# A place in TensorE's order: the second half's norm sums stand at the second slab behind a mixer, and one short unit further on behind a feed-forward

## Chip, core and metric

One NeuronCore of a Trainium2 chip runs the whole program in one launch. The metric is the device time of that launch in microseconds (us); less is better. "TensorE" is PE in the profile's rows (PEld are its weight loads), "VectorE" DVE, "ScalarE" ACT, "GpSimd" POOL, and SP issues the weight stream's DMAs.

## What is computed

Five transformer layers on 512 tokens of width 1024, all in float32. Four layers have a mixer (differential attention, gated linear recurrence, sliding-window attention, differential attention) and a feed-forward, and each of the two is followed by a layer norm over the 1024 features; then a gate adds an embedding. A fifth layer has RMS norms. Cut to what matters here:

```python
def layer_norm(x, g, b):
    mu = jnp.mean(x32, axis=-1, keepdims=True)
    var = jnp.mean(jnp.square(x32 - mu), axis=-1, keepdims=True)
    y = (x32 - mu) * lax.rsqrt(var + LN_EPS) * g + b
...
    for i in range(DEPTH):                      # 4
        y = mixer_i(h)                          # ends in @ w_out
        h = layer_norm(ALPHA * h + y, ln_g[i, 0], ln_b[i, 0])
        u = jnp.square(jax.nn.relu(h @ w_up[i])) @ w_down[i]
        h = layer_norm(ALPHA * h + u, ln_g[i, 1], ln_b[i, 1])
        h = h + jax.nn.sigmoid(h @ w_ple_gate[i]) * (p[i] @ w_ple[i])
# second block: rms_norm, many projections and a merge, @ w_out, rms_norm, feed-forward, rms_norm
```

## The kernel before

**Layout and precision.** Activations lie with features across the 128 partitions: `h[128, 8, 512]` is 8 chunks of 128 features by 512 tokens. A float32 product is made from three matmuls with the operands split in a high and a low part: `whi*xh + whi*xl + wlo*xh` (L446 to L448 for 512 tokens, L545 to L547 for half of them).

**The weight stream.** SyncE streams the weights as slabs of 1024 x 256 into a ring (`raw<-in_stream`). For each slab GpSimd makes the high part (`high_part`, L424, `whi<-raw`) and VectorE the low part (`low_parts`, L1586, `wlo<-raw,whi`), which raises the semaphore `split_done`. A *unit* is TensorE's work on one slab. `begin_unit` waits for `split_done` of the unit's slab, and for the release of the PSUM banks that the unit before last used.

**The order of the work** is written out by hand, engine by engine; there is no scheduler. Each engine runs its own list in order, and a wait holds all that stands behind it on its engine.

**A norm** runs on two halves of the tokens (256 each), so that TensorE has work meanwhile. `pair(..., made=l)` runs the last two units ahead of norm `l` half by half: both units' first halves, then both units' second halves; each half is 8 chunks of 6 matmuls of 256 columns ("half-matmuls" below). `pair(..., read=l)` does the same with the first two units (slabs) that read what norm `l` makes. For each half, the steps are:

- VectorE adds the units' results into `h` and adds up `s1` (sum of `h`) and `s2` (sum of squares, ScalarE squares) with `sums` (L1692);
- TensorE's `stats` (L522) adds `s1` and `s2` across partitions with one-column matmuls; it waits for the semaphores `s1_added` and `s2_added`;
- VectorE's `norm_scalars` (L1700 to L1713) makes mean and reciprocal deviation, with one square root on ScalarE (L1056), and raises `norm_ready`;
- TensorE's `spread` (L533) waits for `norm_ready` and spreads the two rows over the partitions;
- VectorE (L1725, L1727), ScalarE (L1064, L1067) and GpSimd (L419, `xl<-h,xh`) apply them in five pieces of 1, 1, 2, 2, 2 chunks. In an RMS norm VectorE does GpSimd's part (L1743, L1751).

The first half's pieces let `pair(read=l)` do its units' first halves (semaphores `half_x` or `half_r`, a wait per chunk); the second half's pieces (`xh_ready`, `xl_ready`, a wait at every second chunk) let it do the second halves. VectorE's own list at a border (function `border`) is, for the second half:

```python
half(3, 1)                  # add the last unit's second half into h
sums(l, 3, 1)
low_parts(base + 5)         # wlo of the slab of pair(read)'s second unit
norm_scalars(l, 1)
apply(1, 0)
apply(1, 1)
```

GpSimd's list there has the last three pieces of the first half, then `whi` of the slab after (`base + 6`), then the second half's pieces.

There are eleven norms. Norms 0, 2, 4, 6 stand behind the mixers; `pair(read=0, 2, 4, 6)` reads them. Norms 1, 3, 5, 7 stand behind the feed-forwards; behind them TensorE has four short units, all on one slab: those of `p @ w_ple` (12 matmuls of 512 columns each, L446 to L448 with `ph`), and then the gate's units, which read the norm. Norm 8 stands behind the fourth layer's gate, norm 9 behind the second block's `w_out`, norm 10 ends the program. The change touches `pair` (L548) and the loop over the short units (L865 to L870).

Of the kernel before, what the change touches and what calls it, by code (L numbers as in the profile page):

```python
# [193 lines left out]
def build(nc, stream, xin, pin, pos, vecs, relb, onehot, eye, swap, picks, decay, resets, out):  # L194
    with ExitStack() as ctx:
# [168 lines left out]
        def M(name):  # L364
            if name not in m:
                m[name] = sem(name)
            return m[name]
# [74 lines left out]
        def _(pe):  # L442
# [7 lines left out]
            def begin_unit(u):  # L450

                if u:
                    pe.wait_ge(split_done, PLAN.unit_slab[u] + 1)
                if u >= 2:
                    e, v = PLAN.released(u - 2)
                    pe.wait_ge(rel[e], v)
# [27 lines left out]
            def operand_wait(which, gen, k):  # L484

                if k % 2 == 0:
                    hi, lo = (xh_ready, xl_ready) if which == "x" else (gh_ready, gl_ready)
                    pe.wait_ge(hi, gen * 4 + k // 2 + 1)
                    pe.wait_ge(lo, gen * 4 + k // 2 + 1)
# [3 lines left out]
            def whole_unit(u, which, gen=None, token=False, kn=8, w0=0, operand=None):  # L493
                begin_unit(u)
                op = operand or (X if which == "x" else G)
                for k in range(kn):
                    if gen is not None:
                        operand_wait(which, gen, k)
                    last = token_chunk(u, k, kn, op) if token else feature_chunk(u, k, kn, w0, op)
                last.then_inc(unit_done, 1)  # L500

            def out_chunks(layer, first, end):

                for i in range(first, end):
                    j, k = TAIL[i]
                    u = PLAN.at[f"out{layer}"][1] + j
                    if k == 0:
                        begin_unit(u)
                    operand_wait("x", X_GEN[f"mix{layer}"], k)
                    last = feature_chunk(u, k, 8, 0, X)  # L510
                    if k == 7:
                        last.then_inc(unit_done, 1)

            def stats(l, hf):

                for q, total, sem_ in ((0, s1, M("s1_added")), (1, s2, M("s2_added"))):
                    if q == 0 and l >= 2 * NL:
                        continue
                    pe.wait_ge(sem_, 5 * l + (5 if hf else 3))
                    for t in range(2 * hf, 2 * hf + 2):  # L520
                        for part in range(2):
                            last = nc.tensor.matmul(mix[:, 0, 4 * q + t:4 * q + t + 1], total[:, part, t * P:(t + 1) * P], ones[:, 0:1],  # L522
                                                    start=part == 0, stop=part == 1, skip_group_check=True)
                last.then_inc(M("stats"), 1)

            def spread(l, hf):

                pe.wait_ge(M("norm_ready"), 2 * l + hf + 1)
                for bank, c in ((2, 208), (3, 212)):
                    if bank == 3 and l >= 2 * NL:  # L530
                        continue
                    for t in range(2 * hf, 2 * hf + 2):
                        last = nc.tensor.matmul(mix[:, bank, t * P:(t + 1) * P], small[:, c + t:c + t + 1].broadcast_to([P, P]), ident[:, :],  # L533
                                                start=True, stop=True, skip_group_check=True)
                last.then_inc(M("spread"), 1)

            def half_chunk(u, k, hf, operand, own_banks):

                slot = PLAN.unit_slab[u] % RING
                oh, ol = operand  # L540
                for j in range(2):
                    c = slice(j * P, (j + 1) * P)
                    o = proj[:, 2 * (u % 2) + hf, cols(j)] if own_banks else proj[:, 2 * (u % 2) + j, cols(hf)]
                    wh, wl, ah, al = whi[:, slot, k, c], wlo[:, slot, k, c], oh[:, k, cols(hf)], ol[:, k, cols(hf)]
                    nc.tensor.matmul(o, wh, ah, start=k == 0 and (j if own_banks else hf) == 0, stop=False, skip_group_check=True)  # L545
                    nc.tensor.matmul(o, wh, al, start=False, stop=False, skip_group_check=True)  # L546
                    last = nc.tensor.matmul(o, wl, ah, start=False, stop=k == 7, skip_group_check=True)  # L547
                return last  # L548

            def pair(ua, which, gen, made=None, read=None):  # L550

                ub = ua + 1
                points = {}
                if made is not None:
                    points[(ua, 1, 6 if made == 8 else 4)] = (stats, made, 0)
                    points[(ub, 1, 2 if made == 8 else 0)] = (spread, made, 0)
                if read is not None:
                    points[(ub, 0, 1) if read == 8 else (ua, 0, 4)] = (stats, read, 1)
                    points[(ub, 0, 6 if read == 8 else 0)] = (spread, read, 1)
                for u, hf in ((ua, 0), (ub, 0), (ua, 1), (ub, 1)):  # L560
                    if hf == 0:
                        begin_unit(u)
                    for k in range(8):
                        if (u, hf, k) in points:
                            do, l, half = points[(u, hf, k)]
                            do(l, half)
                        if read is not None and hf == 0:
                            if read < 2 * NL:
                                pe.wait_ge(M("half_x"), 5 * read + PIECE_OF[k] + 1)
                            else:  # L570
                                pe.wait_ge(M("half_r"), 8 * (read - 8) + k + 1)
                        elif gen is not None:
                            operand_wait(which, gen, k)
                        last = half_chunk(u, k, hf, X if which == "x" else G, made is not None)
                    if hf:
                        last.then_inc(unit_done, 1)
                    elif made is not None:
                        last.then_inc(M("half_done"), 1)
# [262 lines left out]
            def ffn(layer):  # L841
                s0, u0 = PLAN.at[f"ffn{layer}"]
                pair(u0, "x", X_GEN[f"ln1{layer}"], read=2 * layer)
                for q in range(4):
                    for j in range(0 if q else 2, 4):
                        whole_unit(u0 + 8 * q + j, "x", X_GEN[f"ln1{layer}"])
                    for j in range(4 if q < 3 else 2):
                        whole_unit(u0 + 8 * q + 4 + j, "g", G_GEN[f"ffn{layer}"] + q)
                pair(u0 + 30, "g", G_GEN[f"ffn{layer}"] + 3, made=2 * layer + 1)

            for layer in range(NL):
                if layer % 3 == 0:
                    da_mixer(layer // 3, layer)
                elif layer == 1:
                    hg_mixer(layer)
                else:
                    sw_mixer(layer)
                s0, u0 = PLAN.at[f"out{layer}"]
                out_chunks(layer, 12, 16)
                pair(u0 + 2, "x", X_GEN[f"mix{layer}"], made=2 * layer)  # L860
                ffn(layer)
                s0, u0 = PLAN.at[f"ple{layer}"]
                pe.wait_ge(M("p_hi"), layer + 1)
                pe.wait_ge(M("p_lo"), layer + 1)
                for j in range(4):  # L865
                    whole_unit(u0 + j, "p", kn=2, w0=2 * j, operand=(ph, plo))
                    if j == 0:
                        stats(2 * layer + 1, 1)
                    if j == 1:
                        spread(2 * layer + 1, 1)  # L870
                s0, u0 = PLAN.at[f"gate{layer}"]
                for j in range(4 if layer < NL - 1 else 2):
                    whole_unit(u0 + j, "x", X_GEN[f"ln2{layer}"])
# [1595 lines left out]
```

## Time and profile before

| | us |
|---|---|
| median of 3 runs | 3822.03 (3817.95 to 3822.07) |
| profiled execution, its own time | 3820.47 |
| its span in the trace | 3818.7 |
| TensorE busy | 3617.2 (95%) |
| VectorE busy | 1932.8 (51%) |
| ScalarE busy | 1017.4 (27%) |
| GpSimd busy | 849.7 (22%) |

The page's chain of waits, followed back from the last instruction, is TensorE for 83% of the span, VectorE for 10%, ScalarE for 5%. TensorE's clock was granted at full speed for 0.978 of the span on average. In the page's rows a group has its busy time, the mean of one instruction, and the idle time of its engine just before it with what ended it. In the timeline a row is start, duration, engine, line, operation, output and inputs, count, and in brackets the idle time before it.

### The profile page before, as it was taken

The numbers are of one execution on the slowest core, as the hardware profiler recorded it, in microseconds if no ns is written. First come the engines' busy times: TensorE is split into PE (matmuls) and PEld (weight loads), VectorE is DVE, ScalarE is ACT, GpSimd is POOL, SyncE is SP. The second block draws the span as 40 slices with busy tenths as digits, with TensorE's granted clock in tenths as the row PEclk, the third lists the DMA queues.
The fourth block names the chain that finished last, engine by engine and source line by source line (L and its number), as shares of the span: only waits on it lengthen the run. The fifth ranks groups of instructions, "written<-read, shape, count | busy, mean of one in ns | idle before, by whom it ended". The sixth has DMA issues, their size and how long they took to land.

```text
span 3818.7 us, 44940 instructions
## 1 busy us (share of the span) xinstructions
PE 3617.2 (95%) x18678; PEld 3044.6 (80%) x18678; DVE 1932.8 (51%) x2501; ACT 1017.4 (27%) x1688; POOL 849.7 (22%) x374
## 2 busy tenths in 40 slices
PE   8989999988889999989999999899999999999998
PEld 6778888877778888758888877888888887788887
DVE  4555335576673336555334555644364436554434
ACT  3552002344431113342001256301032213321102
POOL 2113223210022223113222311222221111212221
PEclk9999999999999999999999999999999999999999
DMA  5312222211112222212222221222212222222222
GB/s 188 106 60 89 92 96 89 89 55 45 45 50 100 99 100 78 94 48 78 100 99 89 100 89 56 83 95 96 99 67 89 78 89 88 89 86 92 99 100 78
DMA packets 57427, 330.12 MB, mean 86 GB/s; under 512 B 5595, under 2 KB 12123, under 8 KB 20492
## 3 DMA queue, kind: packets, MB, share of 16 engines
q1 hardware_dynamic: 44748, 304.28, 22.2%
q10 hardware_dynamic: 12480, 22.96, 1.8%
q8 instruction: 152, 2.49, 0.3%
q14 instruction: 47, 0.39, 0.0%
HBM read 324.45 MB, written 8.80 MB: 87 GB/s over the span
## 4 chain that ended last, share of the span: by engine, by line
PE 83%; DVE 10%; ACT 5%; issue 1%; DMA 1%; POOL 0%; ACTq 0%; DVEq 0%
PE proj L446 22%; PE proj L448 21%; PE proj L447 21%; PE proj L545 2%; PE proj L546 2%; PE proj L547 2%; DVE s L1692 2%; DVE wlo L1586 2%; PE proj L479 2%; PE proj L480 1%; PE proj L481 1%; PE mix L618 1%; PE mix L522 1%; PE mix L644 1%; PE mix L710 1%
## 5 line engine op out<-in xcount | busy, mean ns | idle before, releaser
L424 POOL TENSOR_SCALAR whi<-raw 128x2048 fp32r<-128x2048 f32 x286 | 746.7, 2611 | 2684.1 <-DMA raw<-in_stream 2683.6
L446 PE MATMUL proj<-gh,whi 128*128 128x512 f32 x1968 | 792.1, 403 | 14.4 <-ACT gh L1016 10.4
L448 PE MATMUL proj<-gh,wlo 128*128 128x512 f32 x1968 | 772.3, 392 | 0.0
L447 PE MATMUL proj<-gl,whi 128*128 128x512 f32 x1968 | 772.0, 392 | 0.0
L1586 DVE TENSOR_TENSOR wlo<-raw,whi 128x2048 fp32r<-128x2048 f32 x286 | 704.8, 2465 | 84.1 <-POOL whi L424 73.8
L446 PE MATMUL proj<-xh,whi 128*128 128x512 f32 x1760 | 695.2, 395 | 16.3 <-DVE wlo L1586 6.7
L448 PE MATMUL proj<-xh,wlo 128*128 128x512 f32 x1760 | 687.9, 391 | 0.0
L447 PE MATMUL proj<-xl,whi 128*128 128x512 f32 x1760 | 687.5, 391 | 0.0
L446 PEld LDWEIGHTS proj<-gh,whi 128*128 128x128 f32 x1968 | 373.4, 190 | 110.3 <-issue 20.1
L448 PEld LDWEIGHTS proj<-gh,wlo 128*128 128x128 f32 x1968 | 372.8, 189 | 79.8
L447 PEld LDWEIGHTS proj<-gl,whi 128*128 128x128 f32 x1968 | 373.7, 190 | 77.9 <-issue 3.3
L446 PEld LDWEIGHTS proj<-xh,whi 128*128 128x128 f32 x1760 | 332.1, 189 | 95.2 <-issue 9.3
L447 PEld LDWEIGHTS proj<-xl,whi 128*128 128x128 f32 x1760 | 332.4, 189 | 69.4 <-issue 1.9
L448 PEld LDWEIGHTS proj<-xh,wlo 128*128 128x128 f32 x1760 | 331.8, 189 | 69.6
L1325 ACT ACTIVATE rl<-proj 128x1024 f32<-128x1024 f32 x64 | 65.7, 1027 | 951.3 <-PE proj L448 929.6
L1677 DVE TENSOR_TENSOR h<-h,proj 128x1024 f32<-128x1024 f32 (+1 forms) x76 | 80.0, 1053 | 349.7 <-PE proj L448 327.9
L2090 DVE SCALAR_TENSOR_TENSOR hid<-proj,rl 128x1024 f32<-128x1024 f32 x64 | 78.4, 1225 | 334.6 <-ACT rl L1325 334.5
L545 PE MATMUL proj<-xh,whi 128*128 128x256 f32 x640 | 189.8, 297 | 23.0 <-DVE wlo L1586 13.9
L546 PE MATMUL proj<-xl,whi 128*128 128x256 f32 x640 | 185.8, 290 | 0.0
L547 PE MATMUL proj<-xh,wlo 128*128 128x256 f32 x640 | 185.4, 290 | 0.0
L479 PE MATMUL proj<-whi,gh 128*128 128x256 f32 x512 | 155.2, 303 | 1.0 <-ACT da_q L1110 1.0
L419 POOL TENSOR_TENSOR xl<-h,xh 128x512 fp32r<-128x512 f32 (+1 forms) x80 | 99.2, 1242 | 234.1 <-ACT h L1067 234.1
(301 smaller groups left out, 4664.6 us busy)
## 6 DMA issues: line engine op xcount, KB each, us to landing
raw<-in_stream SPq DMA_DIRECT2D x286, 1024.0 KB, 4.8
da_b<-bias_da ACTq DMA_DIRECT2D x16, 512.0 KB, 3.4
bias_da<-bias_rows ACTq DMA_DIRECT2D x8, 512.0 KB, 9.5
h<-in_x ACTq DMA_DIRECT2D x4, 512.0 KB, 8.8
bias_sw<-bias_table ACTq DMA_DIRECT2D x1, 2048.0 KB, 9.7
pf<-in_p ACTq DMA_DIRECT2D x4, 512.0 KB, 5.4
sw_b<-bias_sw ACTq DMA_DIRECT2D x4, 512.0 KB, 3.7
out_features<-fin SPq DMA_DIRECT2D x8, 256.0 KB, 2.3
```

Of the source, the lines that this page charges most:

```text
L419: nc.gpsimd.tensor_tensor(xl[:, k:k + n, cols(hf)], h[:, k:k + n, cols(hf)], xh[:, k:k + n, cols(hf)].bitcast(F32), ALU.subtract)\
L424: nc.gpsimd.tensor_scalar(whi[:, n % RING], raw[:, n % RING], 1.0, 0.0, ALU.mult, ALU.add).then_inc(hi_done, 1)
L446: nc.tensor.matmul(out, wh, ah, start=first, stop=False, skip_group_check=check)
L447: nc.tensor.matmul(out, wh, al, start=False, stop=False, skip_group_check=check)
L448: return nc.tensor.matmul(out, wl, ah, start=False, stop=last, skip_group_check=check)
L479: nc.tensor.matmul(o, ah, wh, start=k == 0 and st % per == 0, stop=False, skip_group_check=True)
L545: nc.tensor.matmul(o, wh, ah, start=k == 0 and (j if own_banks else hf) == 0, stop=False, skip_group_check=True)
L546: nc.tensor.matmul(o, wh, al, start=False, stop=False, skip_group_check=True)
L547: last = nc.tensor.matmul(o, wl, ah, start=False, stop=k == 7, skip_group_check=True)
L1586: V.tensor_tensor(wlo[:, n % RING], raw[:, n % RING], whi[:, n % RING].bitcast(F32), ALU.subtract).then_inc(*own.sig(split_done))
L1677: ins = V.tensor_tensor(o, o, y, ALU.add)
L2090: V.scalar_tensor_tensor(hid[:, :, :], banks(u), 0.0, rl[:, :, :], ALU.max, ALU.mult).then_inc(*own.sig(rel["dve"]))
```

## The change

For the second half of the tokens, `stats` and `spread` move to a later place in TensorE's list; nothing is added or taken away, and no other engine's list is different.

```diff
                 if read is not None:
-                    points[(ub, 0, 1) if read == 8 else (ua, 0, 4)] = (stats, read, 1)
-                    points[(ub, 0, 6 if read == 8 else 0)] = (spread, read, 1)
+                    points[(ub, 0, 1 if read == 8 else 0)] = (stats, read, 1)
+                    points[(ub, 0, 6 if read == 8 else 4)] = (spread, read, 1)
...
                 for j in range(4):
                     whole_unit(u0 + j, "p", kn=2, w0=2 * j, operand=(ph, plo))
-                    if j == 0:
+                    if j == 1:
                         stats(2 * layer + 1, 1)
-                    if j == 1:
+                    if j == 2:
                         spread(2 * layer + 1, 1)
```

`(ua, 0, 4)` is the first unit, first half, ahead of chunk 4; `(ub, 0, 0)` the second unit, first half, ahead of chunk 0. In `pair`'s loop `begin_unit(u)` stands ahead of the chunks of a unit's first half, and so ahead of a step at its chunk 0. `read=8` keeps its places; `read` 0, 2, 4, 6 and 9 move.

TensorE's list behind the first mixer, at `stats` of the second half (`xh`, `xl` are the parts of the activations, `whi`, `wlo` those of the weights, `s_64` and `s_65` are `s1` and `s2`). Before:

```order
L545 MATMUL proj<-xh,whi 128x256
L546 MATMUL proj<-xl,whi 128x256
L547 MATMUL proj<-xh,wlo 128x256
L522 MATMUL mix<-ones,s_64 128x1 [waits s1_added]
L522 MATMUL mix<-ones,s_64 128x1 x3
L522 MATMUL mix<-ones,s_65 128x1 [waits s2_added]
L522 MATMUL mix<-ones,s_65 128x1 x3
L545 MATMUL proj<-xh,whi 128x256 [waits half_x]
```

and now:

```order
L545 MATMUL proj<-xh,whi 128x256
L546 MATMUL proj<-xl,whi 128x256
L547 MATMUL proj<-xh,wlo 128x256
L522 MATMUL mix<-ones,s_64 128x1 [waits s1_added,banks_read_dve,split_done]
L522 MATMUL mix<-ones,s_64 128x1 x3
L522 MATMUL mix<-ones,s_65 128x1 [waits s2_added]
L522 MATMUL mix<-ones,s_65 128x1 x3
L545 MATMUL proj<-xh,whi 128x256 [waits half_x]
```

The step stands 24 half-matmuls later, and the second unit's waits (`banks_read_dve`, `split_done`) now stand ahead of it.

The same list at `spread` of the second half. Before:

```order
L547 MATMUL proj<-xh,wlo 128x256
L533 MATMUL mix<-ident,small 128x128 [waits norm_ready,banks_read_dve,split_done]
L533 MATMUL mix<-ident,small 128x128 x3
L545 MATMUL proj<-xh,whi 128x256 [waits half_x]
L546 MATMUL proj<-xl,whi 128x256
```

and now:

```order
L547 MATMUL proj<-xh,wlo 128x256
L533 MATMUL mix<-ident,small 128x128 [waits norm_ready]
L533 MATMUL mix<-ident,small 128x128 x3
L545 MATMUL proj<-xh,whi 128x256 [waits half_x]
L546 MATMUL proj<-xl,whi 128x256
```

It stands 24 half-matmuls later too, as far behind `stats` as before, and the second unit's waits are gone from it.

TensorE's list behind the first feed-forward, at `stats` of the second half (`ph` and `plo` are the parts of `p`). Before:

```order
L448 MATMUL proj<-ph,wlo 128x512
L522 MATMUL mix<-ones,s_64 128x1 [waits s1_added]
L522 MATMUL mix<-ones,s_64 128x1 x3
L522 MATMUL mix<-ones,s_65 128x1 [waits s2_added]
L522 MATMUL mix<-ones,s_65 128x1 x3
L446 MATMUL proj<-ph,whi 128x512 [waits banks_read_dve,split_done]
```

and now:

```order
L448 MATMUL proj<-ph,wlo 128x512
L522 MATMUL mix<-ones,s_64 128x1 [waits s1_added]
L522 MATMUL mix<-ones,s_64 128x1 x3
L522 MATMUL mix<-ones,s_65 128x1 [waits s2_added]
L522 MATMUL mix<-ones,s_65 128x1 x3
L446 MATMUL proj<-ph,whi 128x512 [waits banks_read_act,split_done]
```

One short unit of 12 matmuls, the one that waits for `banks_read_dve`, now stands ahead of `stats`, and the next one behind it; `spread` has moved behind that next one.

## Rows read from the trace of the kernel before

**Rows 1.** Page, part 1: busy time and share of each engine.

```profile
PE 3617.2 (95%) x18678; PEld 3044.6 (80%) x18678; DVE 1932.8 (51%) x2501; ACT 1017.4 (27%) x1688; POOL 849.7 (22%) x374
```

**Rows 2.** Waits of TensorE: us in total, times, longest.

```profile
PE mix L522 <- DVE s L1692: 34.6, 14, 4.5
PE proj L545 <- DVE wlo L1586: 19.3, 14, 4.1
```

**Rows 3.** Timeline of TensorE, first mixer's norm (start, duration, idle before).

```profile
294.31 1.60 PE L522 MATMUL mix<-ones,s 128*128 128x1 f32 x8 [2.69 <-DVE s L1692]
296.28 1.87 PE L522 MATMUL mix<-ones,s 128*128 128x1 f32 x8 [0.36 <-DVE s L1692]
298.01 0.56 PE L545 MATMUL proj<-xh,whi 128*128 128x256 f32 x1
...
302.47 1.05 PE L533 MATMUL mix<-ident,small 128*128 128x128 f32 x8
...
313.70 0.36 PE L545 MATMUL proj<-xh,whi 128*128 128x256 f32 x1 [1.55 <-POOL xl L419]
```

**Rows 4.** Timeline of VectorE, the same norm.

```profile
296.14 3.97 DVE L1586 TENSOR_TENSOR wlo<-raw,whi 128x2048 fp32r<-128x2048 f32 x1
300.04 0.15 DVE L1700 TENSOR_SCALAR small<-mix 128x2 f32<-128x2 f32 x1
...
301.25 0.16 DVE L1713 TENSOR_TENSOR small<-small 128x2 f32<-128x2 f32 x1
```

**Rows 5.** Timeline of GpSimd, the same norm.

```profile
292.44 1.26 POOL L419 TENSOR_TENSOR xl<-h,xh 128x512 fp32r<-128x512 f32 x1 [2.57 <-ACT h L1067]
294.41 1.26 POOL L419 TENSOR_TENSOR xl<-h,xh 128x512 fp32r<-128x512 f32 x1 [0.70 <-ACT h L1067]
295.64 2.34 POOL L424 TENSOR_SCALAR whi<-raw 128x2048 fp32r<-128x2048 f32 x1
```

**Rows 6.** Timeline of TensorE, the first half's sums of that norm.

```profile
276.33 1.84 PE L522 MATMUL mix<-ones,s 128*128 128x1 f32 x16
```

**Rows 7.** Stretches: engines' busy time (x count), then PEclk, DMA share, GB/s.

```profile
294.63:301.46 6.83, 6.46 (x31) 6.38 (x31) 6.12 (x8) 0.42 (x2) 3.35 (x2) 0.50 0.00 0
2885.35:2892.17 6.82, 6.82 (x35) 6.82 (x34) 0.33 (x2) 0.20 (x1) 0.00 (x0) 0.50 0.01 4
```

**Rows 8.** Timeline at norm 8: one row of VectorE, then TensorE's.

```profile
2882.16 2.28 DVE L1586 TENSOR_TENSOR wlo<-raw,whi 128x2048 fp32r<-128x2048 f32 x1
...
2884.50 0.39 PE L545 MATMUL proj<-gh,whi 128*128 128x256 f32 x1 [4.01 <-DVE wlo L1586]
...
2885.32 1.67 PE L522 MATMUL mix<-ones,s 128*128 128x1 f32 x8
2886.84 0.56 PE L545 MATMUL proj<-gh,whi 128*128 128x256 f32 x1
...
2892.87 0.60 PE L533 MATMUL mix<-ident,small 128*128 128x128 f32 x4
```

**Rows 9.** Timeline at norm 1, behind the first feed-forward: VectorE, then TensorE.

```profile
657.54 0.69 DVE L1677 TENSOR_TENSOR h<-h,proj 128x512 f32<-128x512 f32 x1
...
666.99 0.16 DVE L1713 TENSOR_TENSOR small<-small 128x2 f32<-128x2 f32 x1
...
660.05 3.84 PE L522 MATMUL mix<-ones,s 128*128 128x1 f32 x16 [3.73 <-DVE s L1692]
...
667.94 1.05 PE L533 MATMUL mix<-ident,small 128*128 128x128 f32 x8
```

**Rows 10.** Timeline at norm 9, behind w_out: VectorE, then TensorE.

```profile
3409.22 2.28 DVE L1586 TENSOR_TENSOR wlo<-raw,whi 128x2048 fp32r<-128x2048 f32 x1
...
3421.96 0.48 DVE L1743 SCALAR_TENSOR_TENSOR xl<-tln,vec,xh 128x256 fp32r<-128x256 f32 x1
...
3409.35 1.87 PE L522 MATMUL mix<-ones,s 128*128 128x1 f32 x8 [4.49 <-DVE s L1692]
...
3415.50 0.60 PE L533 MATMUL mix<-ident,small 128*128 128x128 f32 x4
```

## The prediction, made before the changed kernel ran

> **What bounds the kernel now.** I read the page first: TensorE is busy for 95% of the span [rows 1], so only its idle time and its time at half clock can be won or lost. The list of waits says where it idles: 34.6 us stand in front of `stats`, waiting for VectorE's sums, and 19.3 us in front of half-matmuls, waiting for a low weight part [rows 2]. The change moves the first kind of wait; the reader should keep the second kind in mind. Then the timelines at one border of each sort.
>
> At the first mixer's norm, TensorE reaches `stats` of the second half, idles 2.69 us for `s1` and 0.36 more for `s2`, and starts half-matmuls again at 298.01 [rows 3]. From 294.63 to 301.46 its clock is granted at 0.50, that is 1.2 instead of 2.4 GHz [rows 7]: it fell right behind that idle time, and the 24 half-matmuls up to `spread` (298.01 to 302.47) take 4.5 us. Meanwhile VectorE makes the next `wlo` from 296.14 for 3.97 us, starts `norm_scalars` at 300.04 only, and has them done at 301.4 [rows 4]. So `spread` at 302.47 is late by a microsecond, because of TensorE, and everything of the second half hangs on it. Its end can be read: at 313.70 TensorE stops 1.55 us for a piece from GpSimd [rows 3], 11.23 us after `spread` began. From there on it has work without a gap. So **what a norm behind a mixer costs is set by the start of `spread` plus 11.23 us**, not by how much idle time is filled in between.
>
> **The change, norms behind the mixers (four).** Ahead of `stats` now stand the first unit's last 24 half-matmuls. Their inputs come at 293.7 and 295.7 [rows 5], so TensorE works them off in two lots (12 half-matmuls at about 0.12 us are 1.4 us) and is done at about 297.2. VectorE's sums are ready by then (296.28 is when the second sums start now [rows 3]). But the second unit's `begin_unit` now stands ahead of `stats`, and it waits for the low part of that unit's slab, the very `wlo` that VectorE makes right behind its sums, until 296.14 + 3.97 = 300.11 [rows 4]. Before, that wait was hidden behind `stats` and 24 half-matmuls. Queued behind it now are `stats`, then VectorE's `norm_scalars` (until here ready to go when `wlo` ended), then `spread`, then VectorE, ScalarE and GpSimd for the whole second half.
>
> The price of what follows the wait: `stats` took 1.84 us at full clock [rows 6], and 1.60 + 1.87 = 3.5 us in two lots mostly at half [rows 3]. The 24 half-matmuls between `stats` and `spread` (longer than the 1.4 us of `norm_scalars`) take 3.3 us by the six at nearly full clock in rows 8 (2884.50 to 2885.32), and 4.8 us by the thirty at half clock (2886.84 to 2892.87, 0.20 each). So `spread` starts between 300.1 + 1.8 + 3.3 = 305.2 and 300.1 + 3.5 + 4.8 = 308.4, against 302.47: **2.7 to 5.9 us later**. The nearest case is norm 8, whose `stats` already stand behind such a wait: 4.01 us idle, ended by `wlo` (2882.16 + 2.28), and the clock at half from 2885.35 to 2892.17 [rows 7, 8]. By its rates the two steps take 3.0 + 4.8 = 7.8 us here. Of the sixteen sums at the first mixer the first eight took 1.60 us against the last eight's 1.87, part of them still at full clock [rows 3]; for that I take off 0.8 and forecast 7.0 us, so 307.1, 4.6 us late. The second half's chain of 11.23 us behind `spread` keeps its length, and TensorE only has more idle time in it. Four norms: **+18.5 us** (10.8 to 23.6).
>
> A rule of the notes bears on the 3.97 us. The row shows `wlo` at 3.97 us when GpSimd's `whi` began 0.50 us before it [rows 4, 5], and 2.28 us alone [rows 8]. The Trainium skill ("SBUF — State Buffer", Who interferes with whom) says that VectorE's two-input operations and GpSimd share one pair of ports, and that who begins first holds it for the whole instruction. If VectorE won that race here, `wlo` would end at 298.4 and each of the four norms would come 1.7 us earlier, 11.7 us instead of 18.5. Nothing in the change moves either start, so the sum keeps 3.97.
>
> **Norms behind the feed-forwards (four).** Before `stats`, TensorE idled 3.73 us, and its sixteen sums took 3.84 us [rows 9] instead of 1.84 [rows 6]; `spread` began at 667.94, 0.8 us behind the end of `norm_scalars` at 667.15 [rows 9]. Now one short unit stands ahead. It waits for its banks, which VectorE's `add_unit` frees at 657.54 + 0.69 = 658.2; its 12 matmuls end at about 661, `stats` at about 663, another unit at about 666. Its slab is that of all four short units, long split. So `spread` should wait for `norm_scalars`, at 667.2. These stand behind a `wlo` and don't move. One short unit less lies behind `spread`, but the pieces arrive 0.8 us earlier and TensorE then waits for them. Gain about 1 us each, at the fourth some more; no gain at all if the clock falls all the same. **-4.5 us** (-6 to +1).
>
> **Norm 9.** TensorE idled 4.49 us there; 2.9 us of work goes into that, then the wait for `wlo` until 3409.22 + 2.28 = 3411.5 [rows 10]. With 0.9 to 1.9 us of `stats` and 3.3 to 4.8 us of half-matmuls `spread` begins at 3415.7 to 3418.2; I take 3417.5, 2.0 later than 3415.50. Here the pieces come faster: chunk 5's low part ended 6.9 us behind `spread` [rows 10], while TensorE had 72 half-matmuls (9 us) to do until then. It has 24 fewer now, so chunk 4 of the second half starts at 3417.5 + 6.9 = 3424.4, as before (3415.9 + 8.6 = 3424.5): **0 us** (-2 to +1).
>
> **Sum:** +18.5 - 4.5 + 0 = +14 us. From the profiled execution's 3820.47 that is 3834.5; the median of the runs is 1.6 higher, so 3836 for the median.
>
> **The rivals.**
> - *The wait for the slab is hidden, and the change does what it looks like* (faster). Then `stats` start at 297.2, end at about 299, and `spread` begins at about 301.8, bounded by `norm_scalars`: 0.7 us won at four norms, 4 us at norm 9, 4.5 behind the feed-forwards: 3811. It decides if `wlo` ends by 297.2; against it speaks that VectorE has it behind the sums and that norm 8's row shows this very wait [rows 8]. 6%.
> - *The clock stays at 2.4 GHz behind the new wait.* Then each mixer's norm costs the lower bound of 2.7, norm 9 gains 2, the feed-forwards 6: 3822 + 11 - 2 - 6 = 3825, no change that can be told. Against it: the clock was at 0.50 behind the idle times at both norms of rows 7. 5%. The Trainium skill ("TensorE: Matmul & The Clock Gate", Why this matters for your kernels) asks for no long gaps between bursts of matmuls; by it, filling the first gap would help, and the new gap would take that back.
> - *The half clock also strikes in the second half's chain*, where TensorE now stops three times for pieces instead of once. Another low stretch costs 1.5 us or more where TensorE is the bound; at three or four norms +6: 3842. 12%.
> - *VectorE wins the port race* (above): 3829. 3%.
>
> **The numbers.** My forecast has 74%. Its own bounds, taken together without all four norms at one end, give +6 to +21; with the rivals the range is 3827 to 3846. A measurement can tell about 0.2%, 7.6 us, from no change: faster 6%, the same 7%, slower 87%.
>
> **What would show it.** In the changed profile: the wait for `wlo` in front of `stats` (L522) behind each mixer, some 2.9 us; `norm_scalars` no longer right behind `wlo` but 2 to 3.5 us after it; `spread` some 4.6 us later, counted from the same sums; `wlo` still 3.97 us. Behind the feed-forwards a wait for `norm_scalars` (L1713) in front of `spread`. If `stats` behind the mixers don't wait for `wlo`, or `norm_scalars` start right at its end, the forecast is wrong; if the second half's pieces arrive less than 11 us behind `spread`, it is too high.

## The result and the profile after

The changed kernel takes 3838.46 us (median of 5 runs, 3835.62 to 3843.06) against 3821.74 for the kernel before (5 runs, 3816.22 to 3822.07): ratio 1.0049, 95% interval 1.0035 to 1.0063, **18.7 us slower** (13 to 24). The medians lie 16.7 us apart; the ratio is taken over all runs, and 18.7 us is what it makes of the median before. The differences of the experiments below are taken the same way, each against the kernel before as it ran beside them. The forecast was 3836.0, range 3827 to 3846.

The page's first part for the changed kernel, span 3836.6 us:

```profile
PE 3617.2 (94%) x18678; PEld 3038.3 (79%) x18678; DVE 1927.0 (50%) x2501; ACT 1016.8 (27%) x1688; POOL 848.7 (22%) x374
```

TensorE's busy time is the same as in [rows 1]; the span has grown by idle time. The clock's total doesn't explain the loss: it stood at half speed for 152.8 us of this span, for 168.7 us before. (The 0.978 given for the kernel before is the mean granted share, not the share of time at full speed; that was 0.956.) TensorE's list of waits says which idle time grew (us in total, times, longest):

```profile
PE proj L545 <- POOL xl L419: 27.3, 20, 2.1
PE proj L545 <- DVE wlo L1586: 19.4, 14, 4.1
...
PE mix L522 <- DVE wlo L1586: 11.3, 5, 4.0
...
PE mix L533 <- DVE small L1713: 5.0, 4, 1.3
...
PE mix L522 <- DVE s L1692: 2.2, 1, 2.2
```

The sums' wait for VectorE's sums, 34.6 us in [rows 2], is down to 2.2. In its place stand a wait of the sums for `wlo` (11.3 us, five times: four mixers and norm 9), a wait of the spread for the norm scalars (four times: the feed-forwards), and 27.3 us of half-matmuls waiting for GpSimd's pieces, the row to look at. In the kernel before it was

```profile
PE proj L545 <- POOL xl L419: 9.2, 8, 1.6
```

and the 18.1 us more are about what the span has grown by (17.9). The first mixer's norm on TensorE:

```profile
291.26 0.58 PE L545 MATMUL proj<-xh,whi 128*128 128x256 f32 x1 [2.13 <-POOL xl L419]
...
297.69 3.46 PE L522 MATMUL mix<-ones,s 128*128 128x1 f32 x16 [1.91 <-DVE wlo L1586]
305.57 1.05 PE L533 MATMUL mix<-ident,small 128*128 128x128 f32 x8
310.60 0.35 PE L545 MATMUL proj<-xh,whi 128*128 128x256 f32 x1 [1.10 <-POOL xl L419]
313.51 0.36 PE L545 MATMUL proj<-xh,whi 128*128 128x256 f32 x1 [1.25 <-POOL xl L419]
316.77 0.36 PE L545 MATMUL proj<-xh,whi 128*128 128x256 f32 x1 [1.60 <-POOL xl L419]
```

and on VectorE:

```profile
293.66 3.98 DVE L1586 TENSOR_TENSOR wlo<-raw,whi 128x2048 fp32r<-128x2048 f32 x1
301.19 0.16 DVE L1700 TENSOR_SCALAR small<-mix 128x2 f32<-128x2 f32 x1 [3.56 <-PE mix L522]
```

This norm lies 2.5 us earlier in this trace than in the other (its first half's sums start at 273.84, there at 276.33 [rows 6]). Two things are to be read. VectorE, which used to go from `wlo` straight into its norm scalars [rows 4], now stands idle 3.56 us, for it waits for sums that themselves waited for `wlo`. And TensorE has three stops in the second half's chain instead of one: the chain is as long as before, 316.77 - 305.57 = 11.20 us (11.23 in [rows 3]), and whatever was done ahead only leaves it idle there.

Its clock in that norm (stretches: length, busy time of PE, PEld, DVE, ACT and POOL with counts, then PEclk, DMA share, GB/s):

```profile
291.02:294.43 3.41, 3.17 (x15) 3.17 (x16) 2.78 (x3) 1.33 (x3) 2.71 (x3) 0.50 0.00 0
294.43:297.85 3.42, 1.51 (x13) 1.31 (x12) 3.21 (x1) 0.00 (x0) 1.07 (x1) 1.00 0.00 0
297.85:304.67 6.82, 6.82 (x33) 6.82 (x34) 0.98 (x6) 0.20 (x1) 0.00 (x0) 0.50 0.00 0
```

It is at 1.2 GHz twice: in the first 15 of the half-matmuls that now fill the gap, and again from the moment the wait ends until just before the spread.

Behind the first feed-forward:

```profile
661.43 0.47 PE L446 MATMUL proj<-ph,whi 128*128 128x512 f32 x1 [2.05 <-DVE h L1677]
664.27 1.89 PE L522 MATMUL mix<-ones,s 128*128 128x1 f32 x16
670.31 1.16 PE L533 MATMUL mix<-ident,small 128*128 128x128 f32 x8 [1.27 <-DVE small L1713]
675.50 0.47 PE L446 MATMUL proj<-xh,whi 128*128 128x512 f32 x1 [1.26 <-ACT po L1365]
678.88 0.47 PE L446 MATMUL proj<-xh,whi 128*128 128x512 f32 x1 [0.39 <-POOL xl L419]
```

The sixteen sums take 1.89 us instead of 3.84 [rows 9], TensorE waits 1.27 us for the norm scalars, and the spread is bounded by VectorE. From the first half's spread to the second's the granted clock was 0.84, 0.84, 0.84 and 0.79 at these four norms before, and is 1.00 at all four now. At norm 9:

```profile
3428.59 1.87 PE L522 MATMUL mix<-ones,s 128*128 128x1 f32 x8 [3.96 <-DVE wlo L1586]
3435.20 0.60 PE L533 MATMUL mix<-ident,small 128*128 128x128 f32 x4
3442.27 0.36 PE L545 MATMUL proj<-xh,whi 128*128 128x256 f32 x1 [0.72 <-DVE xl L1743]
```

**Where the time went, norm by norm.** I measure each norm in the timelines in two ways: from the first half's spread to the second half's ("spread to spread"), and from the first half's spread to the start of the matmul that stands 400 matmuls behind it, sums and spreads not counted ("stretch"), which takes in what is won back later.

| | spread to spread, before | after | stretch, before | after |
|---|---|---|---|---|
| norms 0, 2, 4, 6 (mixers) | 21.5, 22.2, 21.6, 21.3 | 27.1, 27.1, 27.2, 27.1 | 77.7, 78.4, 77.8, 77.6 | 83.3, 83.2, 83.4, 83.3 |
| norms 1, 3, 5, 7 (feed-forwards) | 21.2, 21.6, 21.2, 22.3 | 20.5 four times | 94.9, 95.7, 94.9, 82.9 | 94.3, 94.7, 94.2, 82.0 |
| norm 9 | 19.9 | 22.7 | 73.9 | 74.8 |

The mixers cost 21.8 us, the feed-forwards give 3.1, norm 9 costs 0.9. Norm 8, where nothing moved, has 1.0 more; it has between 65.0 and 66.0 in all eleven traces of this study, by where the clock falls. That makes +20.6, and the start lies 2.5 us earlier, where nothing was changed either; the spans differ by 17.9.

### The profile page after: what moved, and what is told of

Read it like the earlier page. It is cut to its first block, busy times and chain, and to the rows that moved or that the text cites. A ratio compares the mean times of both kernels' runs of the same rounds, so it can differ in the third digit from the quotient of the medians.

```text
span 3836.6 us, 44940 instructions
## 1 busy us (share of the span) xinstructions
PE 3617.2 (94%) x18678; PEld 3038.3 (79%) x18678; DVE 1927.0 (50%) x2501; ACT 1016.8 (27%) x1688; POOL 848.7 (22%) x374
## 4 chain that ended last, share of the span: by engine, by line
PE 80%; DVE 11%; ACT 6%; issue 1%; DMA 1%; POOL 1%; ACTq 0%; DVEq 0%
PE proj L446 21%; PE proj L448 21%; PE proj L447 21%; DVE wlo L1586 3%; PE proj L545 2%; PE proj L546 2%; PE proj L547 2%; DVE s L1692 2%; PE proj L479 1%; PE proj L480 1%; PE proj L481 1%; PE mix L618 1%; ACT xh L1064 1%; ACT h L1067 1%; PE mix L644 1%
## 5 line engine op out<-in xcount | busy, mean ns | idle before, releaser
L1586 DVE TENSOR_TENSOR wlo<-raw,whi 128x2048 fp32r<-128x2048 f32 x286 | 706.8, 2472 | 89.2 <-POOL whi L424 78.8
L446 PEld LDWEIGHTS proj<-gh,whi 128*128 128x128 f32 x1968 | 373.0, 190 | 110.1 <-issue 20.5
L447 PEld LDWEIGHTS proj<-gl,whi 128*128 128x128 f32 x1968 | 373.4, 190 | 77.6 <-issue 3.4
L446 PEld LDWEIGHTS proj<-xh,whi 128*128 128x128 f32 x1760 | 332.6, 189 | 107.6 <-issue 18.8
L2090 DVE SCALAR_TENSOR_TENSOR hid<-proj,rl 128x1024 f32<-128x1024 f32 x64 | 78.4, 1225 | 334.7 <-ACT rl L1325 334.6
L545 PE MATMUL proj<-xh,whi 128*128 128x256 f32 x640 | 195.2, 305 | 42.1 <-POOL xl L419 27.3
L545 PEld LDWEIGHTS proj<-xh,whi 128*128 128x128 f32 x640 | 132.0, 206 | 48.7 <-DVE wlo L1586 16.7
```

Of the source, the lines that this page charges most:

```text
L446: nc.tensor.matmul(out, wh, ah, start=first, stop=False, skip_group_check=check)
L447: nc.tensor.matmul(out, wh, al, start=False, stop=False, skip_group_check=check)
L1586: V.tensor_tensor(wlo[:, n % RING], raw[:, n % RING], whi[:, n % RING].bitcast(F32), ALU.subtract).then_inc(*own.sig(split_done))
L2090: V.scalar_tensor_tensor(hid[:, :, :], banks(u), 0.0, rl[:, :, :], ALU.max, ALU.mult).then_inc(*own.sig(rel["dve"]))
```

## The experiments

The theory: the loss is the second unit's wait for its slab, which now stands ahead of the sums. The rivals: the later place itself, with the clock that falls in the filled gap; or another of the moved norms.

**Only the norms behind the mixers.**

```diff
-points[(ub, 0, 1) if read == 8 else (ua, 0, 4)] = (stats, read, 1)
-points[(ub, 0, 6 if read == 8 else 0)] = (spread, read, 1)
+points[(ub, 0, 1) if read == 8 else (ua, 0, 4) if read == 9 else (ub, 0, 0)] = (stats, read, 1)
+points[(ub, 0, 6 if read == 8 else 0 if read == 9 else 4)] = (spread, read, 1)
```

> Only the four norms behind the mixers are moved; norm 9 and the feed-forwards stand as before. My theory (the slab's wait now stands ahead of the sums): about +22 us against the kernel before, 5.5 us at each of the four norms, counted from the spread of the first half to the spread of the second (27.1 us against 21.5). Rival (the loss comes from somewhere else, norm 9 or the order on other engines): clearly under +15 us.

Measured 1.0063 (1.0048 to 1.0078), +24 us (18 to 30), as expected. Spread to spread 27.1, 27.9, 26.9, 26.9; stretches 83.1 to 84.5. The whole loss is here.

**Only the norms behind the feed-forwards** (the second part of the change's diff alone).

> Only the norms behind the feed-forwards are moved. My theory: a gain of about 3 us in all (0.6 to 1.0 at each of the four), spread of the second half 0.7 us or more earlier and bounded by VectorE's norm scalars. Rival (what looks like a gain there is only where the clock's low stretch happened to fall): within 1 us of the kernel before in the stretches behind the four norms.

Measured 0.9992 (0.9982 to 1.0001), -3 us, which the timing alone hardly tells from nothing. In the trace the first three have spread to spread 20.6, 20.5, 20.6 and the fourth 19.0; the stretches are 0.6, 1.0, 0.6 and 2.8 us shorter than before. At the first three they are as steady in the other traces that have just this part of the change (94.2 to 94.3, 94.7, 94.2 to 94.3), while the unmoved ones scatter (norm 1: 94.9, 94.9, 95.5 and 96.3 us in four traces). So a gain of some 0.6 to 1 us at each of these is real. The fourth scatters when moved too (80.1 to 82.0), and this trace is of the fastest of the ten runs; its 2.8 us are not to be relied on.

**Only norm 9** (as the first, with `read == 9` moved and the mixers not).

> Only norm 9 is moved. My theory: about +1 us, not to be told from the kernel before by its time; in the trace the second half's spread stands 22.7 us behind the first half's (19.9 before), and 2 of these 2.8 us are given back by the 24 half-matmuls that no longer lie behind it. Rival (the wait costs its full length there too): +2.8 us or more in the stretch.

Measured 1.0006 (0.9997 to 1.0016). Spread to spread 22.7, stretch 74.9 against 73.9: as expected.

**The place without the wait:** all moved as in the change, but `pair` runs the sums just ahead of `begin_unit(ub)`.

```diff
+                    if (u, hf, -1) in points:
+                        do, l, half = points[(u, hf, -1)]
+                        do(l, half)
                     if hf == 0:
                         begin_unit(u)
```

> All norms moved as in the change, but the sums stand ahead of begin_unit of the second unit, so that no wait for the slab stands ahead of them. My theory (the slab's wait is the cause): the loss goes; spread of the second half 21 us or less behind the first half's at the mixers, VectorE's norm scalars start right at the end of wlo again, norm 9 gains up to 4 us; in all 3 to 10 us below the kernel before. Rival (the later place itself and the clock at half speed there are the cause): still +10 us or more.

Measured 1.0023 (1.0013 to 1.0034), 9 us *above* the kernel before (5 to 13). Neither expectation held, though the interval reaches the rival's 10. At the first mixer's norm on TensorE:

```profile
292.65 0.39 PE L545 MATMUL proj<-xh,whi 128*128 128x256 f32 x1 [2.13 <-POOL xl L419]
...
297.11 1.84 PE L522 MATMUL mix<-ones,s 128*128 128x1 f32 x16
303.54 1.05 PE L533 MATMUL mix<-ident,small 128*128 128x128 f32 x8
```

and its clock:

```profile
293.17:296.58 3.41, 3.41 (x18) 3.41 (x18) 2.81 (x2) 0.57 (x2) 3.28 (x2) 0.50 0.00 0
296.58:299.99 3.41, 3.29 (x29) 3.20 (x29) 3.05 (x5) 0.20 (x1) 0.30 (x1) 1.00 0.00 0
299.99:303.41 3.42, 3.42 (x18) 3.42 (x17) 0.33 (x2) 0.00 (x0) 0.00 (x0) 0.50 0.00 0
```

The sums have no wait at all, but the gap is filled at 1.2 GHz, and the 24 half-matmuls up to the spread run at 1.2 GHz again. Spread to spread is 23.7, 23.7, 22.2, 23.7 and the stretches 79.9, 79.9, 78.4, 79.9: 1.7 us more than before in the mean. So most of the loss (5.4 us a norm) is gone with the wait, and the place by itself still costs something. The third norm shows what the second low stretch is worth: there the clock fell only once (1740.42 to 1743.83), and spread and stretch come 1.5 us earlier than at the others. The four stretches (+6.6), the feed-forwards (-4.4) and norm 9 (-0.1) of this trace add up to +2 us, not 9. Part of that is the execution that was profiled, the fastest of the nine (3819.11, median 3823.66); the rest is open.

**The wait without the place:** the kernel before, with one wait added.

```diff
+                    slab_wait = (ua, 0, 4) if read < 8 else None
...
+                        if (u, hf, k) == slab_wait:
+                            pe.wait_ge(split_done, PLAN.unit_slab[ub] + 1)
                         if (u, hf, k) in points:
```

> The kernel before, with nothing moved; only a wait for the second unit's slab put ahead of the second half's sums behind the four mixers. My theory (the wait is the larger part, the later place with its clock the smaller): +3.5 to +5.5 us at each of the four, spread to spread 25 to 27.5 us against 21.5 to 22; +14 to +22 us in all. Rival (the place is the larger part, as the run with the sums ahead of begin_unit would read if the wait cost little alone): under +2 us at each, under +8 in all.

Measured 1.0059 (1.0045 to 1.0073), +23 us (17 to 28), at the upper end of the theory's 14 to 22 and far from the rival's under 8; 5.2 us a norm in the trace, in the 3.5 to 5.5 expected. Its first mixer's norm and its list of waits (L1589 is the old L1586):

```profile
299.38 3.57 PE L522 MATMUL mix<-ones,s 128*128 128x1 f32 x16 [8.55 <-DVE wlo L1589]
307.09 1.05 PE L533 MATMUL mix<-ident,small 128*128 128x128 f32 x8
318.33 0.35 PE L545 MATMUL proj<-xh,whi 128*128 128x256 f32 x1 [1.56 <-POOL xl L419]
```

```profile
PE mix L522 <- DVE wlo L1589: 32.3, 4, 8.6
```

This is the plainest result of the study. Here TensorE idles 8.55 us ahead of the sums, in the changed kernel 2.13 and 1.91, yet the stretches are 83.1, 83.0, 82.9 and 83.6, as with the whole change (83.3). Once the sums wait for the slab, it doesn't matter whether 24 half-matmuls are done ahead or behind: the end is the wait's end, plus the sums and the 24 half-matmuls that stand between them and the spread in both kernels, plus 11.2 us (318.33 - 307.09). Wait and place, each alone and together:

| mean stretch behind the mixers, us | sums don't wait for the slab | they wait |
|---|---|---|
| old place | 77.9 | 83.2 |
| new place | 79.5 | 83.3 |

The 77.9 is of one trace. The same four norms, unmoved, have means of 77.5 and 78.2 in the traces of the feed-forwards' and norm 9's runs, so the place alone costs 1.3 to 2.0 us, and the wait at least 5.0.

**What makes `wlo` long.** GpSimd's list is changed in the changed kernel, so that `whi` of the next slab comes behind the second half's pieces instead of ahead of them.

```diff
-                norm_at[NORM_SLABS[l] + 7] = (l, 1, (0, 1, 2, 3, 4))
+                late[NORM_SLABS[l] + 6] = (l, 1, (0, 1, 2, 3, 4))
...
                 if n in norm_at:
                     low_parts(*norm_at[n])
+                if n in late:
+                    low_parts(*late[n])
                 high_part(n)
```

> The changed kernel, and on GpSimd the next slab's whi goes behind the second half's pieces, so that it no longer runs beside VectorE's wlo. If wlo's 3.97 us are the two engines' shared ports: wlo takes 2.3 us, the wait ahead of the sums ends 1.7 us earlier, and the second half's spread comes 1 to 2 us earlier behind each mixer (about 25.5 us behind the first half's instead of 27.1), in all 4 to 12 us less than the changed kernel. If the 3.97 us have another cause: wlo and the spread stay, time as the changed kernel or worse.

Measured 1.0031 (1.0019 to 1.0044), +12 us, so 7 less than the change. (Lines are 2 later in this kernel.)

```profile
295.23 2.28 DVE L1588 TENSOR_TENSOR wlo<-raw,whi 128x2048 fp32r<-128x2048 f32 x1
```

```profile
297.56 1.95 PE L524 MATMUL mix<-ones,s 128*128 128x1 f32 x16
303.82 1.05 PE L535 MATMUL mix<-ident,small 128*128 128x128 f32 x8
...
315.71 0.36 PE L547 MATMUL proj<-xh,whi 128*128 128x256 f32 x1 [0.30 <-POOL xl L419]
```

```profile
PE proj L448 <- DVE wlo L1588: 19.7, 6, 6.8
```

`wlo` takes 2.28 us instead of 3.98, so GpSimd's `whi` had made it long. The Trainium skill ("SBUF — State Buffer", Who interferes with whom) has it that a VectorE instruction with two inputs in SBUF and a GpSimd instruction that reads SBUF contend for one pair of ports, and the one that began first keeps them. The trace before agrees: 2.28 us from the end of `whi` at 297.98 [rows 5] is 300.26, and `wlo` ended at 300.11 [rows 4]. TensorE no longer idles ahead of the sums. Spread to spread is 23.8, 23.7, 23.6, 23.8, stretches 79.2 four times, 4.1 us less each. That is more than the 1.7 us of `wlo`. The sums ran at full clock too (1.95 us against 3.46), and the chain behind the spread is 0.7 us shorter: its last stop, at chunk 6, comes 11.9 us behind the spread, where chunk 6 stood at 12.6 in the changed kernel (316.77 and 12 half-matmuls on, 1.4 us). In the changed kernel VectorE's next `wlo` (312.77 to 315.50) runs beside GpSimd's last pieces, and two of them take 3.82 us together; here that `wlo` comes at 317.46 and they take 1.29 us each. The last row shows the price (10.7 us in two waits in the changed kernel): behind the feed-forwards the gate's second slab comes late, and those stretches are 1.5 to 2.0 us longer than in the changed kernel.

**The sums inside the gap.** Feed-forwards as in the change; behind the mixers the sums after 12 of the 24 half-matmuls, ahead of the slab's wait, and the spread 18 behind them.

```diff
+points[(ub, 0, 1) if read == 8 else (ua, 0, 7) if read == 9 else (ua, 0, 6)] = (stats, read, 1)
+points[(ub, 0, 6 if read == 8 else 2 if read == 9 else 1)] = (spread, read, 1)
```

> The norms behind the feed-forwards as in the change. Behind the mixers the sums stand ahead of chunk 6 of the first unit (12 half-matmuls into the gap, no slab's wait ahead) and the spread ahead of chunk 1 of the second unit (18 half-matmuls less behind the sums than before the change); at norm 9 ahead of chunk 7 and of chunk 2. My theory: spread at the mixers about 20.5 to 21 us behind the first half's (21.5 to 22 before), a gain of about 1 us each, 4 to 5 us behind the feed-forwards, 1 to 3 at norm 9: in all 8 to 12 us below the kernel before. Rival (the filled gap brings the clock's low stretch forward, as with the sums ahead of begin_unit): no gain at the mixers, in all 4 us or less.

(The expectation says "18 half-matmuls less behind the sums"; the edit puts the spread 18 behind them instead of 24, so 6 less.) Measured 0.9974 (0.9965 to 0.9983), -10 us, in the theory's 8 to 12. But in the profiled execution the mixers gave nothing: stretches 79.1, 76.8, 77.6, 79.2, a mean of 78.2 against 77.9. The clock goes with them; from spread to spread it was granted at 0.79, 1.00, 0.84 and 0.80. The first two of these:

```profile
277.59:300.08 22.49, 19.65 (x128) 19.25 (x127) 18.34 (x23) 9.57 (x19) 10.06 (x7) 0.79 0.26 94
1108.41:1128.92 20.51, 15.99 (x128) 15.09 (x126) 18.35 (x23) 9.57 (x19) 10.24 (x7) 1.00 0.31 103
```

So the rival was right on the mixers in this execution, and wrong in its 4 us for the whole. This execution had the lowest mean clock of the eleven (0.980, 3813.64 us); the five fastest (3803.55 to 3808.91 us) had 0.984 or 0.985, and no trace of them is kept. What the trace does show as gained is the feed-forwards' 4.2 us and 1.4 us at norm 9.

**The same with `whi` late**, and the spread behind the mixers right behind chunk 7, ahead of `begin_unit`.

> As the run with the sums in the gap, with the spread ahead of begin_unit behind the mixers, and whi behind the second half's pieces on GpSimd. If the shared ports are the cause of the 3.97 us: norm_scalars begin 1.7 us earlier at all eight layer norms, spread to spread 19 to 19.5 us behind the mixers, 1 to 1.7 us more behind the feed-forwards: 15 to 22 us below the kernel before. If not, or if wlo of the slab after comes too late for the third unit: 0 to 10 us below.

Measured 0.9976 (0.9967 to 0.9986), -9 us: under the 15 to 22 expected, in the 0 to 10 put down for a `wlo` that comes too late. Stretches behind the mixers 74.4, 74.4, 77.4, 77.2, a mean of 2.0 below before; the granted clock from spread to spread was 1.00, 1.00, 0.81 and 0.82. Norm 9 is 2.5 below; the feed-forwards are 1.0 to 3.1 above at three of four, as with `whi` late before.

**And `whi` late only behind the mixers.**

```diff
+                (norm_at if l % 2 else late)[NORM_SLABS[l] + (7 if l % 2 else 6)] = (l, 1, (0, 1, 2, 3, 4))
```

> As the run with the sums in the gap and whi late, but whi goes late only behind the mixers; behind the feed-forwards GpSimd keeps its old order, since whi late made the gate's second slab come late there. My theory: about 2 us won at each of the four mixers (spread to spread 19 to 21), 4 to 5 us behind the feed-forwards, 1.5 to 2.5 at norm 9: 12 to 16 us below the kernel before, and below the sums in the gap alone. Rival (the gain at the mixers is only where the clock fell in one profiled run): no better than the run with the sums in the gap, 9 us below.

Measured 3801.56 us (6 runs) against 3817.73 for the kernel before beside it, ratio 0.9953 (0.9940 to 0.9967): **18 us below the kernel before** (16 by the medians), better than both kernels, and a little beyond the 12 to 16 us expected, though the interval (13 to 23) reaches into them. Its first mixer's norm (its lines are 2 to 5 later):

```profile
295.09 2.07 PE L524 MATMUL mix<-ones,s 128*128 128x1 f32 x16
298.64 1.16 PE L535 MATMUL mix<-ident,small 128*128 128x128 f32 x8
...
308.66 0.36 PE L547 MATMUL proj<-xh,whi 128*128 128x256 f32 x1 [0.24 <-POOL xl L419]
310.63 0.36 PE L547 MATMUL proj<-xh,whi 128*128 128x256 f32 x1 [0.31 <-POOL xl L419]
```

```profile
294.76 2.28 DVE L1591 TENSOR_TENSOR wlo<-raw,whi 128x2048 fp32r<-128x2048 f32 x1
297.20 0.16 DVE L1705 TENSOR_SCALAR small<-mix 128x2 f32<-128x2 f32 x1 [0.16 <-PE mix L524]
298.42 0.16 DVE L1718 TENSOR_TENSOR small<-small 128x2 f32<-128x2 f32 x1
```

`wlo` and sums end together (297.04, 297.16), the norm scalars follow at once and end at 298.58, the spread starts right behind them, 19.1 us behind the first half's (18.8, 20.8 and 19.1 at the others). Stretches: mixers 74.6, 74.4, 77.1, 74.7, with the clock at 0.91, 1.00, 0.83 and 0.91 from spread to spread; feed-forwards as in the change or up to 1 us shorter; norm 9 71.2. Against the run with the sums in the gap, two things are changed at once behind the mixers, GpSimd's order and a spread 6 half-matmuls earlier; how the gain splits between them is not tried.

## Why the prediction was right, step by step

- *The wait for the slab moves ahead of the sums, and the norm scalars, the spread and the second half's chain queue behind it.* Shown: by its row, by the idle VectorE behind `wlo`, and by the run that adds this wait alone and costs as much as the whole change.
- *7.0 us from the end of the wait to the spread.* It is 305.57 - 297.69 = 7.9 us. This is the term that was sized too small: norm 8's rates gave 3.0 + 4.8 = 7.8, and the 0.8 us taken off for a part at full clock is the whole error. The stretch at half clock began right at the end of the wait (297.85) and took in nearly all sums (3.46 us for 16) and half-matmuls. The norm scalars, done at 302.58, no longer bound the spread; the 24 half-matmuls did. 4.6 us a norm were forecast, 5.4 came; 21.8 us for the four instead of 18.5.
- *The wait begins at 297.2 (2.9 us idle).* It was 1.9 us idle: the filled gap ran at 1.2 GHz, which I had put at 0.12 us per half-matmul. That cost nothing here, since the wait's end doesn't depend on it.
- *The chain of 11.23 us keeps its length.* 11.20.
- *`wlo` keeps its 3.97 us.* 3.98, so the rival in which VectorE wins the race for the ports didn't come; that `whi` is what makes it long is shown by moving `whi`.
- *Feed-forwards: 1 us each, the spread bounded by the norm scalars.* The mechanism was right, a wait of 1.27 us on them; 3.1 us against the one trace before. Against the mean of the four kernels that have these norms as before (95.4, 96.1, 95.3 and 82.7 us) it is 4.2, near the forecast 4.5. Where I had TensorE wait for the pieces, it waited first for ScalarE to empty the banks (`po`, until 675.50). GpSimd's second piece came at 675.30, so that cost little beyond the pieces.
- *Norm 9: spread 2.0 us later, nothing in the end.* 2.8 later, +0.9. The same term again: from the end of the wait to the spread it is 6.6 us (3428.59 to 3435.20), forecast 6.0. TensorE then stops for a piece 7.1 us behind the spread, forecast 6.9, so what the spread loses beyond the 2.0 stays lost.
- *The sum, +14 us.* In the traces the change's own parts make +19.6: the four norms are 3.3 dearer than forecast, the feed-forwards give 1.4 less and norm 9 costs 0.9. All three miss to the same side. The earlier start (-2.5) and norm 8 (+1.0) take 1.5 off and are no part of the change, so that the median came within 2.5 us of the forecast is partly luck.
- *The rival in which the clock stays at 2.4 GHz* fell: behind the wait it was granted at 0.50 (297.85 to 304.67). *The rival in which the clock falls once more in the second half's chain* didn't come: the four low stretches end ahead of the second half's spread, the latest at 1140.94 with the spread at 1141.02, and none follows in the chain. The gain of the *rival with the wait hidden* (0.7 us per mixer's norm) didn't come even where the wait is taken away, and the rows put that down to the clock: with the sums ahead of `begin_unit` the norm scalars were done at 300.4 and the spread began at 303.5, held by half-matmuls at 1.2 GHz, and the place cost 1.7 us. I had priced that rival at full clock.

## What to carry to other kernels

When a step is moved in a list kept by hand, look at which waits it now stands behind, not only at how much work it now stands behind. Here the slab's wait had been harmless for as long as the sums stood ahead of it, because VectorE makes that slab's low part between its own sums and the norm scalars that need TensorE's: the move tied the two into a chain. Where a chain of fixed length hangs on one step, filling idle time ahead of it is worth nothing; only an earlier start of that step is. Here the largest step to it came with GpSimd's order (4.1 us a norm in the changed kernel), on an engine that is busy for 22% of the span.

## What was not expected of the hardware

- Work that fills a gap can itself be slow. With the gap of [rows 3] split in two idle times (2.13 and 1.91 us), the clock fell all the same, 1.1 us earlier counted from the first half's spread (12.5 us behind it instead of 13.7), and a second time behind it. In the kernel before it fell once between the two spreads of a mixer's norm. It doesn't always fall: in the traces of the last three runs, 4 of the 12 mixers' norms have no low stretch between their spreads, and they are the shortest of their traces (76.8 us; 74.4 and 74.4; 74.4).
- A short stop removed can be worth more than its length: 1.7 us less of `wlo` on VectorE became 4.1 us in the stretch, 1.5 of them because TensorE's sums came at full clock. That the clock stayed up because the idle time ahead of the sums was gone is read off the trace only, and not tried by itself.
